# A transformer layer's output projection as three rounded-part products of 512 columns, its weights split anew for every tile

## What is computed

```
o_mla = jnp.einsum('bshc,chv->bshv', o_lat, w_uv).reshape(B, S, MLA_WIDTH)
o_hg, s_new = _hgrn2(hq, hf, hi, hg, lb, hg_gnorm, s0)
h = h + jnp.concatenate([o_mla, o_hg], axis=-1) @ w_o          # w_o: 1024 x 1024
h = h + _hier_moe(_rmsnorm(h, ffn_norm), w_rg, b_rg, w_re, b_re, w1, w3, w2)
```

## Time and profile before

| | |
|---|---|
| median of 3 runs | 1338.44 us (1333.46 to 1340.39) |
| the profiled execution, its own time | 1335.42 us |
| its span | 1333.7 us |
| PE busy | 1133.2 us (85%) |
| DVE / ACT / POOL busy | 716.0 / 507.1 / 313.9 us |

### The profile page before, as it was taken

The page is one execution under the profiler, slowest core; times in us unless marked ns, Lnnn a source line. Parts: engine busy times, 40 slices in busy tenths (PEclk is TensorE's granted clock), DMA queues, the critical chain, the costliest instruction groups (busy, mean ns, idle before and its releaser), DMA issues.

```text
span 1333.7 us, 18558 instructions
## 1 busy us (share of the span) xinstructions
PE 1133.2 (85%) x5999; PEld 920.9 (69%) x5999; DVE 716.0 (54%) x1327; ACT 507.1 (38%) x910; POOL 313.9 (24%) x274
## 2 busy tenths in 40 slices
PE   4999999978988898989899999964898889999910
PEld 3889899944566777777777786753676767777700
DVE  3430510156555545555454544446777877788736
ACT  3334221133222222121322232305777777777612
POOL 2100400000000000000000000004665656666546
PEclk9999999979997989998999999986999999999965
DMA  6340141151132011110101000005788776764278
GB/s 242 108 147 0 56 131 46 52 138 40 33 110 64 27 57 49 32 64 17 64 17 63 17 35 22 32 32 190 262 283 280 254 270 221 263 227 157 80 289 293
DMA packets 97107, 158.93 MB, mean 119 GB/s; under 512 B 13760, under 2 KB 66448, under 8 KB 97040
## 3 DMA queue, kind: packets, MB, share of 16 engines
q1 hardware_dynamic: 84272, 113.49, 25.2%
q0 software_dynamic: 11680, 42.47, 9.2%
q10 hardware_dynamic: 1088, 2.10, 0.4%
HBM read 167.81 MB, written 40.55 MB: 156 GB/s over the span
## 4 chain that ended last, share of the span: by engine, by line
PE 58%; DVE 11%; DMA 10%; issue 9%; ACT 7%; SPq 2%; POOL 2%; POOLq 0%; ACTq 0%; DVEq 0%
PE ps L934 9%; DMA below<-in_w 6%; PE ps L901 5%; PE ps L773 4%; PE ps L791 4%; PE ps L1942 4%; PE ps L1944 4%; PE ps L1943 4%; DVE low L1619 3%; PE ps L860 3%; ACT high L1334 2%; PE ps L1937 2%; PE ps L1936 2%; PE ps L1938 2%; SPq L1227 2%
## 5 line engine op out<-in xcount | busy, mean ns | idle before, releaser
L1619 DVE TENSOR_TENSOR low<-below,high 128x1024 fp32r<-128x1024 f32 x128 | 196.7, 1584 | 72.1 <-ACT high L1334 62.8
L1800 POOL TENSOR_SCALAR arena<-arena 128x1 f32<-128x1 f32 (+5 forms) x38 | 16.5, 434 | 718.8 <-ACT arena L761 323.1
L1295 POOL TENSOR_TENSOR low<-below,high 128x1024 fp32r<-128x1024 f32 x64 | 148.5, 2339 | 106.9 <-ACT high L1355 106.9
L1432 PE MATMUL ps<-high 128*128 128x512 f32 x384 | 157.9, 411 | 15.1 <-DVE low L1629 11.1
L1434 PE MATMUL ps<-high,low 128*128 128x512 f32 x384 | 152.9, 398 | 0.0
L1433 PE MATMUL ps<-low,high 128*128 128x512 f32 x384 | 152.6, 397 | 0.0
L567 ACT ACTIVATE arena<-ps 128x512 f32<-128x512 f32 (+7 forms) x109 | 56.9, 531 | 236.4 <-PE ps L773 235.9
L1334 ACT ACTIVATE high<-below 128x1024 fp32r<-128x1024 f32 x128 | 129.1, 1051 | 44.0 <-DMA below<-in_w 44.0
L934 PE MATMUL ps<-arena 128*128 128x256 f32 (+1 forms) x576 | 130.4, 379 | 3.8 <-ACT arena L567 3.6
L934 PEld LDWEIGHTS ps<-arena 128*128 128x128 f32 (+1 forms) x576 | 105.2, 184 | 28.6 <-ACT arena L747 5.6
L773 PE MATMUL ps<-arena 128*128 128x128 f32 (+4 forms) x613 | 99.9, 290 | 10.1 <-ACT arena L753 3.1
(11 more groups left out here) (215 smaller groups left out, 1991.2 us busy)
## 6 DMA issues: line engine op xcount, KB each, us to landing
below<-in_w SPq DMA_DIRECT2D x256, 256.0 KB
below<-in_w POOLq DMA_DIRECT2D x64, 512.0 KB
y_dram<-arena SPq DMA_DIRECT2D x32, 512.0 KB, 2.9
arena<-in_x_prompt SPq DMA_DIRECT2D x16, 512.0 KB
below<-in_w_in SPq DMA_DIRECT2D x12, 512.0 KB, 6.9
out<-arena SPq DMA_DIRECT2D x9, 512.0 KB, 5.3
arena<-in_w_o SPq DMA_DIRECT2D x4, 1024.0 KB, 9.4
h_dram<-arena SPq DMA_DIRECT2D x8, 512.0 KB, 2.6
```

The lines of the kernel that those rows point to most:

```text
L1295: pool.tensor_tensor(w2_lo[s % UN][:, c], w2_in[:, c], w2_hi[s % UN][:, c].bitcast(F32), ALU.subtract).then_inc(s_w2lo, 1)
L1432: pe.matmul(out, x_hi, w_hi, start=start, stop=False)
L1619: dve.tensor_tensor(chunk(w13_lo[j], c), chunk(w13_in, c), chunk(w13_hi[j], c).bitcast(F32), ALU.subtract).then_inc(s_w13lo, 1)
```

## The change

- The output projection becomes two halves of 512 columns. For each of 8 contraction chunks three float32r matmuls are issued (24 for a half, 48 for a tile). The first half is a step at head 3, the second at head 7 of the next turn (heads 2 and 5 in turn 8).
- `w_o` is no longer resident. POOL loads raw blocks of 128 x 512 (256 KB) into a ring of four (`wo_raw`). A step `ws` splits one block: ACT waits for the raw block and for the place in `wo_hi` and writes the rounded part; POOL waits for it, writes `wo_lo`, waits for its own result, and issues the load of the block four further on. One half is resident at a time (`wo_hi`, `wo_lo`), so all 16 blocks are loaded and split for every tile, 144 in all. The second half of the last tile has a place of its own (`last_hi`, `last_lo`), which is free after the last score.
- The places of the `ws` steps for the common turn: first half, blocks 0 and 1 behind `attn` 7, 2 and 3 behind `ho` (ahead of `qt`), 4 and 5 behind head 0, 6 and 7 behind head 1; second half, blocks 0 to 2, 3 to 5, 6 and 7 behind heads 4, 5 and 6. In turn 8: tile 7's second half behind heads 3 and 4; the last tile's own 16 blocks in fours behind head 6, head 7, `attn` 6 and `attn` 7.
- In `wot` ACT now copies both groups (rounded, `mix_hi`) and DVE subtracts both (`mix_lo`); before, each copied one.
- `sq` and `hn` move behind `attn` 6 and `attn` 7. The ring of probability rows goes from three to two. ACT's `ho` also waits for the rope of the same tile, since `o_sq` lies on `rope_tmp`. SP loads `fn_b` later and no longer loads `w_o`. Most buffers get other places.

```
 X_RING = 4
+WO_RING = 4
...
-    wo_base = r.at
-    wo = r.take(KC, D)
-    wo_end = r.at
...
-    p_rows = r.take(3, D)
...
+    wo_raw = Region(r.at, below, below_floats).take(WO_RING, 512)
...
+    hi, lo = Region(0, high, parts_floats), Region(0, low, parts_floats)
+    wo_hi, mix_hi = hi.take(KC, 512), hi.take(KC, P)
...
+    last_hi = Region(parts_floats - KC * 512, high, parts_floats).take(KC, 512)
+    last_lo = Region(0, low, parts_floats).take(KC, 512)
...
+    wo_lo, mix_lo = lo.take(KC, 512), lo.take(KC, P)
...
+    q_t = r.take(MH, P)
+    o_sq = Region(r.at).take(HH, HK)
+    rope_tmp = r.take(4, MH * 16)
+    p_base = r.at
+    p_rows = r.take(2, D)
...
-    WO_PARTS = 4
+    WO_PARTS = 2
+
+
+    def wo_split(i, half, chunks):
+        return [("ws", i, half * KC + c) for c in chunks]
+
+    WO_AT = [{3: 0, 7: 1}] * (NT - 1) + [{2: 0, 5: 1}]
+    WO_SPLIT_AT = [{0: (-1, 0, range(4, 6)), 1: (-1, 0, range(6, 8)), 4: (-1, 1, range(0, 3)), 5: (-1, 1, range(3, 6)),
+                    6: (-1, 1, range(6, 8))}] * (NT - 1)
+    WO_SPLIT_AT += [{0: (-1, 0, range(4, 6)), 1: (-1, 0, range(6, 8)), 3: (-1, 1, range(0, 4)),
+                     4: (-1, 1, range(4, 8)), 6: (0, 0, range(0, 4)), 7: (0, 0, range(4, 8))}]
     KN = [(0, 512), (512, 512), (1024, T + PAST - 1024)]
     KB_OF = [range(0, 4), range(4, 8), range(8, KB)]
     STEPS = [("kb", kb, 0) for kb in KB_OF[2]] + [("hs", 0, 0)]
@@ -416,20 +436,34 @@
             STEPS.append(("score", i, hd))
             if i == 0 and hd != 6:
                 STEPS.append(("v", hd, 0))
-            side = {1: "wot", 6: "sq", 7: "hn"}.get(hd)
+            side = ({1: "wot"} if i + 1 < NT else {1: "wot", 6: "sq", 7: "hn"}).get(hd)
             if hd == 0:
                 STEPS.append(("hf", i, 0))
             if i and side:
                 STEPS.append((side, i - 1, 0))
-            if i and 2 <= hd < 2 + WO_PARTS:
-                STEPS.append(("wo", i - 1, hd - 2))
+            if i and hd in WO_AT[i]:
+                STEPS.append(("wo", i - 1, WO_AT[i][hd]))
             if hd == 6 and i + 1 < NT:
                 STEPS.append(("q", i + 1, 0))
             if i + 1 < NT and hd < rounds(i + 1):
                 STEPS.append(("h", i + 1, hd))
             if hd >= 2:
                 STEPS.append(("attn", i, hd - 2))
-        STEPS += [("attn", i, 6), ("attn", i, 7)]
+            if i and hd in WO_SPLIT_AT[i]:
+                w, half, chunks = WO_SPLIT_AT[i][hd]
+                STEPS += wo_split(i + w, half, chunks)
+        STEPS.append(("attn", i, 6))
+        if i + 1 == NT:
+            STEPS += wo_split(i, 1, range(0, 4))
+        elif i:
+            STEPS.append(("sq", i - 1, 0))
+        STEPS.append(("attn", i, 7))
+        if i + 1 == NT:
+            STEPS += wo_split(i, 1, range(4, 8))
+        else:
+            STEPS += wo_split(i, 0, range(0, 2))
+            if i:
+                STEPS.append(("hn", i - 1, 0))
         if i:
             STEPS.append(("hnt", i - 1, 0))
         if i + 1 < NT:
@@ -437,6 +471,7 @@
         STEPS.append(("mpv", i, 0))
         if i + 1 < NT:
             STEPS.append(("ho", i + 1, 0))
+            STEPS += wo_split(i, 0, range(2, 4))
             STEPS.append(("qt", i + 1, 0))
             if i + 2 < NT:
                 STEPS.append(("hs", i + 2, 0))
...
+        if kind == "wot":
+            for key in keys:
+                g, half = PT_GROUP[key], key[3]
+                src = ps[:, 4 + g % 2, :].rearrange("p (a b) -> p a b", a=4)[:, :, 0:R]
+                some = slice(4 * half, 4 * half + 4)
+                if who == "act":
+                    eng.wait_ge(s_pt, g + 1)
+                    eng.activation(mix_hi[:, some, 0:R], src, ACT.Copy).then_inc(s_mixhi, 1)
+                else:
+                    eng.wait_ge(s_mixhi, 2 * i + half + 1)
+                    eng.tensor_tensor(mix_lo[:, some, 0:R], src, mix_hi[:, some, 0:R].bitcast(F32),
+                                      ALU.subtract).then_inc(s_ptrel[g % 2], 1)
+            return
         for key in keys:
             if not copies_it(key, who):
                 continue
...
                     ins.then_inc(rel, 1)
+
+    def wo_at(i, half):
+
+        return (last_hi, last_lo) if i + 1 == NT and half else (wo_hi, wo_lo)
+
+    def wo_free(i, half):
+
+        if i + 1 == NT and half:
+            return S_JOB[("score", i, MH - 1)]
+        if half:
+            return S_JOB[("wo", i, 0)]
+        return S_JOB[("wo", i - 1, 1)] if i else max(S_JOB[st] for st in STEPS if st[0] in ("kn", "v"))
 
     def attention_loads(sp):
         def load_fq(i):
...
-        sp.wait_ge(s_sps2, max(S_JOB[st] for st in STEPS if st[0] in ("kn", "v")) + 1)
-        w = D // WO_PARTS
-        for part in range(WO_PARTS):
-            sp.dma_start(wo[:, :, part * w:(part + 1) * w],
-                         w_o[0, :, part * w:(part + 1) * w].rearrange("(c p) n -> p c n", p=P)).then_inc(s_wo[part], 16)
         for i in range(NT):
             t, R = ORDER[i], ROWS[ORDER[i]]
             if i + 2 < NT:
...
+
+        def load_wo(n):
+            half, c = divmod(n % (2 * KC), KC)
+            pool.dma_start(wo_raw[:, n % WO_RING, :],
+                           w_o[0, c * P:(c + 1) * P, half * 512:(half + 1) * 512]).then_inc(s_woraw[n % WO_RING], 16)
+
+        for n in range(WO_RING):
+            load_wo(n)
         for st in STEPS:
-            kind, i, _ = st
+            kind, i, hd = st
+            if kind == "ws":
+                n = 2 * KC * i + hd
+                half, c = divmod(hd, KC)
+                w_h, w_l = wo_at(i, half)
+                pool.wait_ge(s_wohi, n + 1)
+                pool.tensor_tensor(w_l[:, c, :], wo_raw[:, n % WO_RING, :], w_h[:, c, :].bitcast(F32),
+                                   ALU.subtract).then_inc(s_wolo, 1)
+                if n + WO_RING < 2 * KC * NT:
+                    pool.wait_ge(s_wolo, n + 1)
+                    load_wo(n + WO_RING)
             if st == ("score", 0, 0):
                 pool.wait_ge(s_wr, 32)
                 pool.wait_ge(s_fnc, 16)
...
+            if kind == "ws":
+                n = 2 * KC * i + hd
+                half, c = divmod(hd, KC)
+                act.wait_ge(s_woraw[n % WO_RING], 16 * (n // WO_RING + 1))
+                act.wait_ge(s_sps2, wo_free(i, half) + 1)
+                act.activation(wo_at(i, half)[0][:, c, :], wo_raw[:, n % WO_RING, :], ACT.Copy).then_inc(s_wohi, 1)
             if st in S_JOB:
                 k = S_JOB[st]
                 bank = s_banks(st)
...
+                    act.wait_ge(s_qrope, i + 1)
                     act.activation(o_row[0:R], ps[0:R, bank, :].rearrange("p (h v) -> p h v", h=HH),
                                    ACT.Copy).then_inc(s_oc, 1)
...
-
-                        act.wait_ge(s_pt, last_group(a - 3) + 1)
-                    act.activation(p_rows[0:R, a % 3, 0:w],
+                    if a >= 2:
+
+                        act.wait_ge(s_pt, last_group(a - 2) + 1)
+                    act.activation(p_rows[0:R, a % 2, 0:w],
                                    ps[0:R, bank:bank + 2, :].rearrange("p a b -> p (a b)")[:, 0:w], ACT.Exp,
                                    bias=nbias[0:R, i % 2, hd:hd + 1], scale=SCALE,
                                    accum_out=sm_stat[0:R, 2, hd:hd + 1]).then_inc(s_srel[k % 2], 1)
...
-                pe.wait_ge(s_wo[hd], 16)
                 pt_wait_done(pe, ("wot", i, 0, 0))
                 pt_wait_done(pe, ("wot", i, 0, 1))
-                w = D // WO_PARTS
+                w_h, w_l = wo_at(i, hd)
+                out = ps[0:R, bank, :]
                 for kc in range(KC):
-                    ins = pe.matmul(ps[0:R, bank, 0:w], mix_t[:, kc, 0:R], wo[:, kc, hd * w:(hd + 1) * w],
-                                    start=kc == 0, stop=kc == KC - 1)
+                    pe.wait_ge(s_wolo, KC * (2 * i + hd) + kc + 1)
+                    x_h, x_l = mix_hi[:, kc, 0:R], mix_lo[:, kc, 0:R]
+                    pe.matmul(out, x_h, w_h[:, kc, :], start=kc == 0, stop=False)
+                    pe.matmul(out, x_h, w_l[:, kc, :], start=False, stop=False)
+                    ins = pe.matmul(out, x_l, w_h[:, kc, :], start=False, stop=kc == KC - 1)
                 ins.then_inc(s_sps2, 1)
             if kind == "hnt":
                 for part in range(WO_PARTS):
```

58 lines of the change are left out of this document (29 added, 29 removed).

## The result

| | before | after |
|---|---|---|
| median of four runs each | 1338.1 us (1333.5 to 1340.4) | 1414.6 us (1411.9 to 1421.0) |
| ratio of the times | 1 | 1.059, 95% interval 1.056 to 1.062 |
| span of the profiled execution | 1333.7 us | 1419.0 us |

The forecast was 1358 us, range 1326 to 1385. The sign was right, the size was not: 57 us more than the sum said are to be explained.

The account below looks back on a forecast made before the run. PE was taken to set the attention phase's pace. The terms -27 + 10 + 6 + 22.8 + 7 + 0 + 2 = +21 us gave 1356.4 or 1359.4 us, stated as 1358 us, range 1326 to 1385.

Parts of the forecast that it names:

- Products: Output projection on PE: 48 float32r matmuls per tile gain 3.04 us for each of nine tiles, -27 us.
- `wot` of turns 1 to 8 has two heads before its use: Mixed rows' split in `wot`: hidden before its use, counted as zero; 0.8 us per turn if that cover were gone.
- Placement: Heads with and without `wo`: fewer score waits (down to -9) against DVE's pace in turns 1 to 3 (up to +5); 0.
- Between turns: Two ACT copies ahead of `qt`'s copy: +7 us (0 to +10); copies behind `attn` 6 and 7: zero, at most +1 a turn.
- POOL and DVE together: Small turns: POOL's subtractions and DVE's instructions sometimes wait for each other, +2 us for DVE (0 to +10).
- Second halves: Second projection halves, turns 1 to 7: PE stalls for POOL's blocks in turns 1 to 4, +10 us (+1 to +34).
- the `q` matmuls on PE cover that: Second halves, turns 1 to 7: ACT is blocked some 4 us at heads 5 and 6, but PE has `q` work meanwhile.
- Turn 8: Tile 7's second half waits for blocks, +6 us (+3.5 to +9.5); last tile's 16 blocks delay the end, +22.8 (+14 to +28).
- the fast one: Whole kernel: block costs 1.7 us or less, ACT hardly held, exponential waits go; -15, some 1323 us, chance 0.2.
- the even one: Whole kernel: a block of 1.8 us and half the delay between turns; +3.5, about 1341 us, chance 0.17.
- Contention: Whole kernel: DVE and POOL hold each other, a block costs 2.6 us, every turn stalls; +56, 1393 us, chance 0.1.

Follow-up runs that it names:

- the third row of the table: New layout, two probability rows and weights split in turn 0, added to the kernel with halves and the mixed rows' split: 1372.6 us, ratio 1.028, step +10.
- one pair of kernels: DVE's mixed-row subtractions moved behind head 1's level work, in the kernel before with halves and the mixed rows' split added: 1336.1 us, was 1364.9.
- in the second: DVE's mixed-row subtractions moved behind head 1's level work, in the changed kernel with weights split only once: 1326.1 us, was 1343.6.
- in the third: DVE's mixed-row subtractions moved behind head 1's level work, in the changed kernel with loads issued by ACT two blocks ahead: 1366.5 us, was 1390.9.

## Why the forecast failed, step by step

Steps of 10 or 12 us in this table are not far above what two kernels can be told apart by; those of 29, 39 and 49 are.

- **Products, -27.** Right: -29. It is seen only when all else stands still, since the split of their own left operand takes more than it.
- **"`wot` of turns 1 to 8 has two heads before its use."** This is the step that failed, and the largest error: 0 in the sum, 0.8 us per turn if the cover were gone, measured +39 by itself; in the kernel with ACT's loads, moving DVE's subtractions gives back 22. I had asked who uses the *result* of `wot` (the product at head 3, with time to spare) and not what is queued *behind* the new instructions on their engine. On DVE that is the level work of head 1, which PE needs at head 2. And it was priced in instruction time alone: the wait for ACT's copies, which stand behind an exponential, and PE at half clock after its stand count as well.
- **Placement, 0 with -9 to +5.** The better end came, or a little more: -11. The waits at scores went as I had hoped, from 8.6 to 2.1 us in turns 1 to 7, but they are not all: those for DVE's copies in front of weighing (L791, L797 there) fell from 8.9 to 2.9, and PE now waits 9.1 us for the level work.
- **Between turns, +7 and at most +1 a turn.** ACT's copies cost 12 us in all: the upper end. The mechanism is there: in turns 1 to 7 of the changed kernel `meta` (L928) stands 5.0 us in five places, up to 1.0 us each, on a wait that the kernel without the copies does not have.
- **POOL and DVE together, +2 (0 to +10).** The subtractions cost 10, the upper end, but the pair was sized without the issues. In the changed kernel the two lines above take 34 us more than without POOL's work, though PE's wait for them did not grow with the issues. This was a rival's mechanism, at a chance of 0.1, though not with its numbers: the block did not get slower (1.98 us, not 2.6), DVE did.
- **Second halves, +10, waiting for POOL.** The products wait only 3.5 us for POOL in the whole phase, and in turns 1 to 7 not at all by the trace. The loads' part of turns 1 to 7 (+19, from 458.9 to 478.1) came out elsewhere. ACT stood 23.9 us in 14 places in front of raw blocks, which I had put at the pace of POOL. PE's scores then wait 12.4 us for exponentials, where the kernel without loads has 3.9; its other waits for ACT are within 1.4 us of that kernel's. PE stands 6 us more in all, and 13 us of the 19 are the same matmuls taking longer at a clock of 0.86 instead of 0.88. That ACT would be held was in the forecast, that PE's scores pay for it was not ("the `q` matmuls on PE cover that").
- **Turn 8, +6 and +22.8.** The second was right, in size and in kind: block pace, ACT's hold, the late exponential of `mpv` and PE at half clock came as worked out (20.3 up to the last `wo`, measured 20.8). The first, with tile 7's product gain, was +3; measured +10.1. The loads' part of it is 7.3 (43.0 without them, 50.3 with them), near the 6 of the sum; the 2.8 that stay without loads, in place of -3, are not that term's but the split's and the copies' (the split of the mixed rows alone takes the score of head 6 from 40.7 to 43.4 us behind `meta`). Its working also took 1.3 us for a score of 1024 columns; the scores and the turns behind them in turn 8 start 1.8 us apart (848.07 and 849.85), which moves the term by only half a microsecond.
- Not settled: the 10 us of the third row of the table (its three parts were not run apart), and how the loads' 19 us of turns 1 to 7 divide between landings and POOL's issues. The kernel with loads by ACT has about 8 of them left, with DVE's lines nearly as in the kernel without loads (57.0 and 15.5 us).

Of the rivals, the fast one fell with its own condition (no block below 1.7 us), and so did the even one. Contention gave 1393 us, nearest in size, by a sum that is not what happened.

## What to carry to other kernels

An instruction added to an engine is paid by whatever stands behind it in that engine's order, and not only by whoever reads its result: look for the next thing on that engine that PE waits for, and put the new work behind it. A wait of PE can have a second price, the stretch at half clock that follows. It varied here: 12.9 us less of waits at the moved place were 29 us of time in one pair of kernels, 14.9 were 22 in the second, 18.9 were 22 in the third. Where one in-order engine both empties a ring and asks for its refill, it should not ask for the place that the engine behind it has just begun to work on: one block of lead less was worth some 100 us here.

## What was not expected of the hardware

DVE instructions with two SBUF inputs stood behind POOL, and not only when POOL's subtraction was running before they began. In turn 6 of the changed kernel:

```profile
672.86 0.56 POOL L750 DMA_DIRECT2D below<-in_w_o  x1 [0.30 <-POOL low L762]
...
673.11 1.47 DVE L1110 TENSOR_TENSOR arena<-arena 128x16 f32<-128x16 f32 x1
...
673.43 1.10 POOL L762 TENSOR_TENSOR low<-below,high 128x512 fp32r<-128x512 f32 x1
...
680.77 0.56 POOL L750 DMA_DIRECT2D below<-in_w_o  x1 [0.30 <-POOL low L762]
...
680.87 0.29 DVE L1042 TENSOR_TENSOR arena<-arena 128x128 f32<-128x128 f32 x1
```

An instruction on 16 columns begins 0.25 us into an issue, with the subtraction still 0.32 us off, and ends with that subtraction, 1.47 us later. One on 128 columns that begins 0.10 us into an issue takes its usual 0.29 us. Over the whole phase, those that begin 0.19 to 0.31 us into an issue with a subtraction behind it take 1.4 to 1.7 us (25 of them). Of nine that begin in its first 0.15 us, eight take their usual time and one, at 0.15, takes 1.83. Of three later ones, at 0.35, 0.41 and 0.55 us, the first takes 0.28, the others 1.57 and 1.30.

The Trainium skill, page "SBUF — State Buffer", section "Who interferes with whom", says that a DVE instruction with two SBUF inputs contends with a GpSimd instruction that reads SBUF, for ports that are an exclusive lock, and that issue order decides who blocks. It adds that a `tensor_tensor` was not seen to stall a DMA issued by GpSimd, and infers that this is because the writing of descriptors needs the other interface of the pair. The second case, an issue beside which the DVE instruction takes its usual time, fits that inference. The first differs from the rule by the recorded starts: the DVE instruction starts first and still waits. Whether the issue's last part holds it or the subtraction queued behind it already does, these rows do not tell.

An issue took ACT 0.33 us and POOL 0.57, and on POOL another 0.30 us of waiting for its own result stood in front of it.
